# Norms put together with the modulation, their inverse root taken of token columns, and the first two weight tiles read side by side

## The reference, cut to what matters

```python
def rmsnorm(x, g):
    y = x * lax.rsqrt(jnp.mean(x * x, axis=-1, keepdims=True) + RMS_EPS)
    return y * g
def modulate(x, shift, scale):
    return x * (1.0 + scale) + shift
def layer_norm(x, g, b):
    mu = jnp.mean(x, -1, keepdims=True)
    var = jnp.mean(jnp.square(x - mu), -1, keepdims=True)
    return (x - mu) * lax.rsqrt(var + LN_EPS) * g + b
# block 1, behind the mixer and around the experts
h_lat = h_lat + g1_l * mix_l
f_l = modulate(rmsnorm(h_lat, norm2), sh2_l, sc2_l)
h_lat = h_lat + g2_l * peer(f_l, ...)
x = rmsnorm(h_lat, final_norm)
# block 2, both layers i, for latent and (in layer 0) context tokens
h_l = xl * (1.0 + sc1_l) + sh1_l                  # into the mixer: even or odd
xl = layer_norm(ALPHA * xl + gt1_l * o_l, ln1_g[i], ln1_b[i])
h_l = xl * (1.0 + sc2_l) + sh2_l                  # into the feed-forward
xl = layer_norm(ALPHA * xl + gt2_l * f_l, ln2_g[i], ln2_b[i])
```

## Time and profile before

| what | value |
|---|---|
| median of 3 runs | 4767.77 us (4763.95 to 4772.82) |
| the profiled execution | 4765.72 us |
| its span (first to last instruction) | 4763.8 us |
| PE busy | 4363.6 us (92%) |
| PEld, DVE, ACT, POOL busy | 3398.6, 2498.6, 1510.1, 1804.2 us |
| moved by DMA | 441.31 MB, mean 93 GB/s |

### The profile page before, as it was taken

One profiled execution on the slowest core, in us unless ns is written; L12 is line 12 of the kernel. 1 busy time (PEld: TensorE's weight loads), 2 busy tenths in 40 slices (PEclk: granted clock), 3 DMA queues, 4 the chain that ended last, 5 costly groups with the idle time before them and its releaser, 6 DMA issues.

```text
span 4763.8 us, 51427 instructions
## 1 busy us (share of the span) xinstructions
PE 4363.6 (92%) x20890; PEld 3398.6 (71%) x20890; DVE 2498.6 (52%) x4227; ACT 1510.1 (32%) x2528; POOL 1804.2 (38%) x987
## 2 busy tenths in 40 slices
PE   7878999987779999999999989997999979988998
PEld 3667755456667888888888866675888857656886
DVE  4675745359868676664544342544344350364334
ACT  3212211034863232323222233543222232353232
POOL 2244423024965444444444413002223315333442
PEclk9998999989889999999999989998999989998999
DMA  5200300321355555454533310001212112102331
GB/s 216 81 27 6 117 27 27 133 85 49 128 199 187 171 172 173 155 177 163 181 129 133 116 62 15 19 19 40 67 63 67 63 31 62 36 1 71 97 93 49
DMA packets 170761, 441.31 MB, mean 93 GB/s; under 512 B 12220, under 2 KB 78972, under 8 KB 167581
## 3 DMA queue, kind: packets, MB, share of 16 engines
q1 hardware_dynamic: 168060, 422.61, 26.1%
q0 software_dynamic: 2464, 15.41, 0.8%
HBM read 402.32 MB, written 35.65 MB: 92 GB/s over the span
## 4 chain that ended last, share of the span: by engine, by line
PE 69%; DVE 6%; POOL 4%; ACT 3%; issue 2%; DMA 0%; POOLq 0%; ACTq 0%; DVEq 0%
PE psum L256 19%; PE psum L254 19%; PE psum L255 19%; PE psum L260 11%; POOL o L1600 2%; PE psum L281 1%; DVE o L1493 1%; POOL Pe L2411 1%; POOL Pd L2413 1%; DVE X L1882 1%; DVE ffl L1822 0%; DVE o L1495 0%; DVE rstd L1862 0%; DVE X L1885 0%; DVE ci L1444 0%
## 5 line engine op out<-in xcount | busy, mean ns | idle before, releaser
L244 POOL TENSOR_TENSOR pair<-raw_ring,pair 128x1024 fp32r<-128x1024 f32 x502 | 1244.4, 2493 | 2010.6 <-ACT pair L236 2010.5
L236 ACT CAST pair<-raw_ring 128x1024 fp32r<-128x1024 f32 x502 | 510.9, 1047 | 368.8 <-PE psum L256 315.7
L254 PE MATMUL psum<-pfh,pair 128*128 128x512 f32 x1152 | 451.6, 392 | 27.6 <-POOL pair L244 26.8
L1675 DVE SCALAR_TENSOR_TENSOR h<-psum,mods,h 128x512 f32<-128x512 f32 x512 | 370.7, 748 | 162.5 <-PE psum L256 160.7
L255 PE MATMUL psum<-pfl,pair 128*128 128x512 f32 x1152 | 449.9, 391 | 0.0
L256 PE MATMUL psum<-pfh,pair 128*128 128x512 f32 x1152 | 449.7, 390 | 0.0
L254 PE MATMUL psum<-ffh,pair 128*128 128x512 f32 (+1 forms) x1056 | 375.8, 356 | 44.9 <-DVE ffl L1822 44.9
L254 PE MATMUL psum<-Ah,pair 128*128 128x512 f32 x1024 | 400.9, 391 | 9.7 <-DVE h L1675 4.9
L255 PE MATMUL psum<-Al,pair 128*128 128x512 f32 x1024 | 400.5, 391 | 0.0
L256 PE MATMUL psum<-Ah,pair 128*128 128x512 f32 x1024 | 400.3, 391 | 0.0
L256 PE MATMUL psum<-ffh,pair 128*128 128x512 f32 (+1 forms) x1056 | 377.7, 358 | 0.0
(11 more groups left out here) (569 smaller groups left out, 8959.6 us busy)
## 6 DMA issues: line engine op xcount, KB each, us to landing
raw_ring<-wmod SPq DMA_DIRECT2D x144, 512.0 KB, 4.7
raw_ring<-peeru SPq DMA_DIRECT2D x128, 512.0 KB, 4.4
raw_ring<-peerv SPq DMA_DIRECT2D x128, 512.0 KB, 3.7
gates<-stage SPq DMA_DIRECT2D x16, 2048.0 KB, 6.4
Gb<-gates SPq DMA_DIRECT2D x32, 1024.0 KB, 9.5
raw_ring<-win SPq DMA_DIRECT2D x48, 512.0 KB, 4.5
raw_ring<-wgate SPq DMA_DIRECT2D x44, 512.0 KB, 3.5
raw_ring<-wup SPq DMA_DIRECT2D x44, 512.0 KB, 3.6
```

Of the source, the lines that this page charges most:

```text
L236: ac.e.copy(self.pair(t)[0], k.R.of(t)).then_inc(*k.A.up("hi", t))
L244: po.e.tensor_tensor(lo, k.R.of(t), hi.bitcast(F), ALU.subtract).then_inc(*k.G.up("lo", t))
L254: e.matmul(out, w[0], x[0], start=first, stop=False, skip_group_check=True)
L1675: e.scalar_tensor_tensor(out=h[:, j, :], in0=B.of(("down", gi, j)), scalar=m[:, 40 + j, 0:1], in1=h[:, j, :], op0=ALU.mult, op1=ALU.add).t ...
```

## The change

1. The inverse root is taken over token columns. The sum over channels comes as one column for each 128 tokens (`tensor_columns`: the squares are the stationary operand, one column of weights moves), so a norm of 512 tokens has 128x4 values in `r8`, one of 768 has 128x6. `vector_column` and `scalar_column` add, take root and reciprocal of these, and `tensor_along` spreads them along the tokens of a PSUM bank again, by a matmul with the column broadcast and the identity.
2. The norm's gain and the modulation are put together. `vector_gains` computes gain, bias and their ALPHA multiples ahead of time; `vector_apply` multiplies by gain and inverse root (PSUM operand) in one instruction, ScalarE adds the bias (`scalar_apply`), `vector_keep` later writes the normed X times ALPHA in place, from a copy `rstd` that ScalarE makes of the bank. `vector_last` and `scalar_last` do the last norm.
3. Remainders 1, 3, 5, 7 (`SECONDS`) are made by GpSimd (`pool_seconds`), from a second pass of ScalarE; the others by VectorE, two tiles behind. Four temporaries in place of two.
4. `project_abreast` reads the first two weight tiles (wq, abin, dqk, gate and up) side by side: for each activation tile q, both names and all segments, all banks taken first.
5. Means and sums: GpSimd sums tiles 0 to 5 (`pool_sum`, `pool_squares`), so TensorE takes three means or sums in place of eight. The variance's matmuls write 64 partitions each, even and odd tiles into different halves of the columns; one ScalarE copy and a column sum with `sel` put the halves together.
6. Squares of norm2 and of the final norm are taken within the stage ahead; additions to the modulation stand before the last tile; the context load is issued from GpSimd's queue earlier; the first weight's split comes ahead of the norm's work.

The diff, cut to its core:

```diff
+def project_abreast(k, pe, names, x, segs, each, among=(0, 1, 2, 3, 4, 5, 6, 7)):
+    for n in names:
+        pe.wait_ge(k.W.split(n))
+        for s in range(len(segs)):
+            k.B.take((n, s), 1, among)
+            pe.wait_ge(k.B.free((n, s)))
+    for q in range(8):
+        qs = slice(128 * q, 128 * q + 128)
+        pe.wait_ge(each(q))
+        for n in names:
+            hi, lo = k.W.pair(n)
+            for s, (a, b) in enumerate(segs):
+                i = trio(pe.e, k.B.of((n, s))[:, 0:b - a], (hi[:, qs], lo[:, qs]), x(q, s), q == 0, q == 7)
...
+SECONDS = (1, 3, 5, 7)
+def second_made(k, key, q):
+    return k.G.at(key, "f", q) if q in SECONDS else k.V.at(key, "f", q)
+def pool_seconds(k, po, key, n, tmp, fh, fl):
+    for j in SECONDS:
+        po.wait_ge(k.A.at(key, "g", j))
+        po.e.tensor_tensor(fl[j][:, 0:n], tmp[j % len(tmp)][:, 0:n], fh[j][:, 0:n].bitcast(F), ALU.subtract).then_inc(*k.G.up(key, "f", j))
+def tensor_columns(k, pe, key, sources, n, w, among=(0, 1, 2, 3, 4, 5, 6, 7)):
...
+            i = mm(pe.e, bank[:, c:c + 1], x[:, 128 * c:128 * c + 128], w, i2 == 0 and c == 0, i2 == len(sources) - 1)
+def tensor_along(k, pe, key, segs, among=(0, 1, 2, 3, 4, 5, 6, 7)):
...
+            i = mm(pe.e, bank[:, 128 * c - a:128 * c - a + 128], k.r8[:, c:c + 1].to_broadcast([128, 128]), k.sq["ident"])
+def vector_column(k, dv, key, n, eps):
+    r = k.r8[:, 0:n]
+    dv.wait_ge(k.P.at(key, "col"))
+    dv.e.tensor_scalar(r, k.B.of((key, "col"))[:, 0:n], eps, None, ALU.add).then_inc(*k.V.up(key, "ms"))
+    dv.wait_ge(k.A.at(key, "sqrt"))
+    dv.e.reciprocal(r, r).then_inc(*k.V.up(key, "r"))
+def pool_squares(k, po, key, total, sq):
+    for j in range(1, 6):
+        po.wait_ge(k.A.at(key, j))
+        po.e.tensor_tensor(total, sq[0] if j == 1 else total, sq[j % 4], ALU.add).then_inc(*k.G.up(key, j))
...
 def scalar_route(k, ac):
     everyone(k, ac, "out")
+    W.hi(ac, ("wq", 0))
+    scalar_column(k, ac, "n2", 4)
...
+def vector_apply(k, dv, key, src, segs, tmp, fh, fl):
+    for j in range(10):
+        if j < 8:
+            x = tmp[j % 4]
+            dv.wait_ge(second_made(k, key, j - 4) if j > 3 else None)
+            for s, (a, b) in enumerate(segs):
+                e.scalar_tensor_tensor(out=x[:, a:b], in0=k.X[:, j, a:b], scalar=c.gain[s][:, j:j + 1], in1=k.B.of((src, "rb", s))[:, 0:b - a],
+                                       op0=ALU.mult, op1=ALU.mult).then_inc(*V.up())
+        i = j - 2
+        if i < 0 or i in SECONDS:
+            continue
+        dv.wait_ge(k.A.at(key, "hi", i))
+            e.scalar_tensor_tensor(out=fl[i][:, a:b], in0=tmp[i % 4][:, a:b], scalar=c.bias[s][:, i:i + 1], in1=fh[i][:, a:b].bitcast(F),
+                                   op0=ALU.add, op1=ALU.subtract).then_inc(*V.up())
...
+def scalar_apply(k, ac, key, src, segs, tmp, fh):
     for j in range(8):
+        ac.wait_ge(k.V.at(key, "x", j))
+            e.activation(fh[j][:, a:b], x[:, a:b], AF.Identity, bias=c.bias[s][:, j:j + 1]).then_inc(*A.up())
+        if j in SECONDS:
+                e.activation(x[:, a:b], x[:, a:b], AF.Identity, bias=c.bias[s][:, j:j + 1]).then_inc(*A.up())
+    for s, (a, b) in enumerate(segs):
+        e.copy(k.rstd[:, a:b], k.B.of((src, "rb", s))[:, 0:b - a]).then_inc(*A.up(key, "rstd", s))
+        k.B.over((src, "rb", s), A.now())
+def vector_keep(k, dv, key, n):
+    dv.wait_ge(k.A.at(key, "rstd", (n - 1) // 512), V.now())
+        e.scalar_tensor_tensor(out=x, in0=x, scalar=c.ga[:, j:j + 1], in1=k.rstd[:, 0:n], op0=ALU.mult, op1=ALU.mult).then_inc(*V.up())
+        e.tensor_scalar(x, x, c.ba[:, j:j + 1], None, ALU.add).then_inc(*V.up())
...
-def tensor_norm(k, pe, key, segs, sqt):
+def tensor_norm(k, pe, key, segs, sqt, total):
-            i = mm(pe.e, k.B.of((key, "var", s))[:, 0:b - a], k.sq["m1024"], sqt[j % 2][:, a:b], j == 0, j == 7)
+            h = slice(64 * ((j + s) % 2), 64 * ((j + s) % 2) + 64)
+            i = mm(pe.e, k.B.of((key, "var", s))[h, 0:b - a], k.sq["m1024"][:, 0:64], sqt[j % 4][:, a:b], j < 2, j > 5)
+    tensor_columns(k, pe, key, [(total, lambda c: k.A.at(key, "sums", c // 4))], n, k.sel, SIX)
+    tensor_along(k, pe, key, segs, SIX)
...
 def tensor_residual(...):
         project_in(k, pe, (wname, j), x3, segs, each if j == 0 else None)
-        if j:
-            tensor_mean(k, pe, key, j - 1, segs, lambda s: k.V.at(key, "res", j - 1, s))
-    tensor_mean(k, pe, key, 7, segs, lambda s: k.V.at(key, "res", 7, s))
+    tensor_mean(k, pe, key, 5, segs, total, lambda s: k.G.at(key, "sum", 5))
+    for j in (6, 7):
+        tensor_mean(k, pe, key, j, segs, total, lambda s: k.V.at(key, "res", j, s))
+def pool_residual(k, po, key, wname, segs, total):
+    for j in range(8):
+        k.W.lo(po, (wname, j))
+        pool_sum(k, po, key, j - 1, segs[-1][1], total, lambda i: k.V.at(key, "res", i, len(segs) - 1))
...
 def vector_odd(k, dv):
-    vector_affine(k, dv, "od", SEG2, f.aff, f.fh, f.fl)
+    vector_apply(k, dv, "od", "ff0", SEG2, f.aff, f.fh, f.fl)
+    vector_keep(k, dv, "od", 512)
     pr, lamb = f.tmp[:, 0:64], k.lamb
```

More of the change, by code:

```diff
@@ L1300, in lay_peer @@
     m.at = low
-    k.fsq = [m.take("fsq", 512) for _ in range(2)]
-    k.frstd = m.take("frstd", 512)
+    m.at = low + 4096
+    k.fsq, k.fsum = [m.take("fsq", 512) for _ in range(4)], m.take("fsum", 512)
 def tensor_route(k, pe):
     e, P, V, A, G, B = pe.e, k.P, k.V, k.A, k.G, k.B
[L1307 to L1312, removed]
+    tensor_columns(k, pe, "n2", squares(k, "sq2", k.psum, k.psq), 4, k.sq["m1024"][:, 0:1])
+    tensor_along(k, pe, "n2", SEG1)
     P.name("end", "norm2")
-    everyone(k, pe, "norm2")
     def scores(n):
@@ L1647, in tensor_experts @@
     P.name("end", "experts")
[L1648 to L1653, removed]
+    tensor_columns(k, pe, "n3", squares(k, "sq3", k.fsum, k.fsq), 4, k.sq["m1024"][:, 0:1])
+    tensor_along(k, pe, "n3", SEG1)
     P.name("end", "first")
@@ L1789, in lay_second @@
     k.rstd = m.take("rstd", 768)
+    k.lnv = {}
+    for key in ("ff0", "od", "ff1"):
+        c = k.lnv[key] = Kernel()
+        c.gain, c.bias = [m.take("lng", 8) for _ in range(2)], [m.take("lnb", 8) for _ in range(2)]
+        c.ga, c.ba = m.take("lnga", 8), m.take("lnba", 8)
     k.top = m.at
@@ L1801, in vector_affine_scale, with vector_gains @@
     k.V.name(key, "one")
-def scalar_affine(k, ac, key, m, j0, segs, tmp, fh, ready):
-    e, A, n = ac.e, k.A, segs[-1][1]
-    ac.wait_ge(k.V.at(key, "one"))
+def vector_gains(k, dv, key, m, j0, segs, g, b):
+    e, V, c = dv.e, k.V, k.lnv[key]
+    for s in range(len(segs)):
+        sc = m[:, j0 + 8:j0 + 16, s]
+        e.scalar_tensor_tensor(out=c.gain[s], in0=sc, scalar=1.0, in1=g, op0=ALU.add, op1=ALU.mult).then_inc(*V.up())
+        e.scalar_tensor_tensor(out=c.bias[s], in0=sc, scalar=1.0, in1=b, op0=ALU.add, op1=ALU.mult).then_inc(*V.up())
+    e.tensor_scalar(c.ga, g, ALPHA, None, ALU.mult).then_inc(*V.up())
+    e.tensor_scalar(c.ba, b, ALPHA, None, ALU.mult).then_inc(*V.up())
+    dv.wait_ge(V.now())
+    for s in range(len(segs)):
+        e.tensor_tensor(c.bias[s], c.bias[s], m[:, j0:j0 + 8, s], ALU.add).then_inc(*V.up())
+    V.name(key, "gains")
@@ L2493, in lay_even @@
     f.sqt = f.P[1:3]
+    f.four = f.P[1:3] + f.PT[0:2]
+    f.behind = [min(7, max(j, (at_in + 768 * (j + 1) - k.base - 8193) // 512)) for j in range(8)]
 def tensor_rms(k, pe, key, n, sq, mean):
```

359 lines of the change are left out of this document (212 added, 147 removed).

## The result

The changed kernel takes 4693.74 us (median of 4 runs, 4686.91 to 4696.24) against 4770.30 us for the kernel before, run beside it on the same chips. The ratio is 0.9837, 95% interval 0.9819 to 0.9856: 77 us less, where 104 were forecast. 4694 lies 4 us above the range.

A forecast was written before the change was run, and what follows sets the result against it. TensorE, holding 69% of the chain, was taken to bound the kernel, with gains only where it idles at six norm joints. Their gains sum to 104 us: 4767.8 less 104 gives 4663.8, forecast 4664, range 4646 to 4690.

The forecast's parts named there:

- A: First of six norm joints, ahead of wq: pair of weight tiles done 23.3 us after the last addition to h; gain 19.8.
- B: Second joint, behind the experts, ahead of abin, context tiles too: pair done at 2814.8, evacuation in a bunch +1.3; gain 17.5.
- C: Third joint, ahead of ff0's gate 0 and up 0: pair done T+57 (T: last matmul ahead); gain 8.4 + 7.8 = 16.2.
- D: Fourth joint, ahead of odd attention's dqk: rotations done T+50.8 (T: last matmul ahead); gain 14.8 + 7.8 = 22.6.
- E: Fifth joint, ahead of ff1's gate and up: pair done T+33.5 (T: last matmul ahead); gain 12.2 + 5.2 = 17.4.
- F: Last joint, final norm to end of span: ends T+22.1 (T: last matmul ahead); gain 5.3 + 5.2 = 10.5.
- The bank wait and the lambda wait: C: first matmul waits for the inverse root's bank, T+38; D: rotation waits for lambda behind vector_keep, T+45.6.
- rival 3: In C or D the bank or the lambda wait isn't there: 4653 us, with both gone 4643; chance 0.12.
- Rival 2: VectorE's remainders in A to E each wait for a GpSimd instruction, some 3 us per joint: 4676 to 4684; chance 0.17.
- Rival 4: Halves of columns run one after the other and columns cost 0.225, 16 us in all: 4680; chance 0.07.
- Rival 5: TensorE's clock stays at 0.50 after the joints: 4768 us and more, up to 4814; chance 0.03.
- Rival 6: No effect, each joint's end set by something unnamed such as weights arriving: 4768 us; chance 0.03.

The follow-up runs named there:

- e10: Changed kernel padded so every distance from weight tile to moving tile is as in the kernel before: 4666.99 us, ratio 0.9793.
- e5: Changed kernel with the rota of PSUM banks moved on before ff0's first gate tile: 4682.67 us, ratio 0.9811.
- e6: Changed kernel with one tile of the odd layer's vector_keep behind each of rotations 1 to 8: 4690.11 us, ratio 0.9839.
- e7: Changed kernel with SECONDS = (), all eight remainders by VectorE: 4692.32 us, ratio 0.9834.
- e4: Kernel before the change with the split weight tiles moved by 64 bytes, moving tiles where they were: 4804.38 us, ratio 1.0069.
- e2: Kernel before the change with 64 bytes of padding ahead of both work areas: 4802.41 us, ratio 1.0081.
- e1: Changed kernel with padding alone, both work areas beginning at byte 128 of 256: 4672.73 us, ratio 0.9792.
- e3: Kernel before the change with block 2's tiles alone moved, from byte 192 of 256 to 128: 4770.90 us, ratio 1.0001.
- e8: Changed kernel with distance 0 in block 1 and ff1, 64 for 768-column tiles, banks moved on, vector_keep behind the rotations: 4647.90 us, ratio 0.9748.
- e9: e8 with SECONDS = () too, all eight remainders by VectorE: 4654.70 us, ratio 0.9765.
- e11: e9 once more, unchanged, one profile: 4654.79 us.
- e12: e6 once more, unchanged, one profile: 4683.41 us.

## Why the prediction was wrong

The step that failed is the sum itself: it took every dense stage at its old pace ("TensorE runs without a gap behind them") and listed as the edits at nothing only instructions. The change also moved SBUF tiles by 64 and 640 bytes, and that cost 21 to 27 us, nearly all in matmuls that it doesn't touch: e10, which differs in padding alone, gains 98 us where 104 were forecast. No rival had it, so no chance stood against it, and the range ended at 4690. That e10's time is within 3 us of 4664 is in part luck: its joints gain 100.8 and not 104, and the kernel before beside it was some 3 us faster than the 4767.8 the forecast started from.

Point by point, forecast and measured gain of each joint in the changed kernel: A 19.8 and 19.7. B 17.5 and 12.8. C 16.2 and 14.3. D 22.6 and 23.2. E 17.4 and 14.2. F 10.5 and 10.4. In all 104 and 94.6. A part of the shortfall is the layout's again, since e10 has 100.8; there B (14.6) and E (15.0) still lack 2.9 and 2.4, and D gives 2.6 more than forecast.

- **B** (forecast 4.7 too much): the column sum waits for GpSimd's last addition and then has 24 instructions, so it ends 1.5 us later than the terms 0.7 and 1 had it; spreading back took 2.06 for 0.9. The price of 0.11 an instruction was too low: 8 of them take 1.17 at full clock (E), 0.15 each, and 2.06 at the low level, 0.26 each. The evacuation of both tiles in a bunch cost 3.2 (the lead falls from 27.2 to 24.0; a weight cast of 1.04 stands in front of it), not 1.3.
- **E** (forecast 3.2 too much): the wait that ended last was GpSimd's, behind three weight remainders of 2.5 each, which puts the end of the pair at T+34.8 for T+33.5. The means that left gave 3.3 for 5.2, partly by the slower pace (4.2 in e10).
- **The bank wait and the lambda wait** (in the forecast, rival 3 against): both in the chain at the forecast place to within 1 us, and worth 10.2 and 10.6 by e5 and e6. Rival 3 falls.
- **Rival 2, the shared port**: where a VectorE instruction with two SBUF inputs meets GpSimd it does wait. The largest wait is C's first remainder, 4.92 us in two instructions (2.43 and 2.56), while GpSimd made three weight remainders; E's first took 2.82. Two of the groups of C's remainders (by line and form, as in the earlier trace rows):

```profile
L1922 DVE SCALAR_TENSOR_TENSOR ffl<-hid,lnb,ffh 128x512 fp32r<-128x512 f32 x2 | 3.2, 1586 | 0.8 <-ACT ffh L1933 0.8
...
L1922 DVE SCALAR_TENSOR_TENSOR ffl<-gacc,lnb,ffh 128x512 fp32r<-128x512 f32 x2 | 2.1, 1075 | 0.2 <-ACT ffh L1933 0.2
```

  The means mix two kinds: one of 2.43 and one of 0.74 in the first group, one of 1.41 and one of 0.74 in the second. So 0.74 is the length without a wait, and waits of 0.5 to 0.8 us beside GpSimd's work come in A, C, D and E too. They do not cost the 3 us a joint of the rival: with GpSimd's half gone (e7) the time is the same, B, C and E gain 1.1 to 1.5 more and D 1.9 less. The Trainium skill's rule ("SBUF — State Buffer", Who interferes with whom) agrees with the 4.92 and the 2.82, and speaks against this change less than it seemed.
- **Rival 4, the halves of columns**: the variance of C takes 7.6 for eight tiles (from 3239.36 in the chain to ScalarE's copy at 3246.99), 0.95 a tile for the 1.32 before, VectorE's pace, as forecast. Column sums of 12 instructions take 1.51, 0.126 each.
- **Rival 5, the clock**: it falls. Full clock is back 5.6 us behind the first matmul in A and 5.5 behind it in C, where the kernel before needed 5.2 and 17.8: there TensorE went on with gaps (0.50 in the 15 us behind C's start), in the changed kernel the pair runs without one, and the same 15 us have 0.82. The windows in the experts, ff0 and ff1 are at 1.00. Rival 6 falls with the gain itself.

The reading that decided the gain was right, and so were the places and mechanisms of the joints; what was missing is a look at what the change moves in memory.

## What to carry to other kernels

A new buffer ahead of others moves all that follow it. Where TensorE is busy without a gap, count matmuls in windows of equal length before and after: a change in their number, with nothing waiting, may come from the layout and not from the change's logic. Then pad, so that moving and stationary tiles keep their distance, and judge the change by that. Profile twice before you read a small difference: ff0's pace changed between two executions of one program.

When a total hardly moves, look at the lead stage by stage: here two experiments won 10 us each in their joint, and a pace that differs from one execution to the next took about half of it back in their profiles.

## What the runs showed of the hardware

- The pace of dense fp32r matmuls depends on the distance of weight tile and moving tile within 256 bytes. Where all have 512 columns it is 0.2267 us at 0, 0.2289 at 64, 0.2324 at 128, 0.2333 at 192. Moving the weight tiles (e4) does the same as moving the others (e2). The cause behind it was not measured.
- Where 512 and 256 columns alternate (ff0) it is another order. The 512-column ones take 0.229 at 0 and 64 and 0.233 at 128 and 192. The 256-column ones take 0.120 at 0 (e1, e3), 0.119 in the mean at 128 (e2, e4), and at 64 0.113 in before, e8 and e10 but 0.118 in e9 and e11. At 192 the same program had 0.118 in one execution and 0.113 in the next (e6, e12). So the distance alone does not fix it.
- Odd attention, whose chain runs through GpSimd, lost 4.5 us in the changed kernel and 2.5 in e10. The same program lost 2.1 in e6 and gained 0.9 in e12, so at least 3 us of such a figure can be the execution's. The rest is open.
